# Moving the sampled rows' output projection into the tail of the convolution, with earlier weight loads, moved threshold steps and a moved first chunk

## The reference, cut to what matters

```
# layer 0
xn = rms_norm(y) ; q, k, v, iq, ik, iw, gate = split(xn @ att_w_in)
score = sum_h iw * relu(iq . ik) ; idx = top_k(score, 256)      # threshold search for the prompt rows,
o = softmax(q . k[idx]) @ v[idx]                                 # repeated extraction of 8 for the sampled rows
y = y + (o * silu(gate)) @ att_w_out                             # 1024 x 1024
# layer 1
xn = rms_norm(y) ; qkv, z, b, a = split(xn @ dn_w_in)            # 1024 x (3072 + 1024 + 16)
qkv = silu(conv4([state_dn_conv, qkv]))                          # new_buf is its last three rows
o = gated_delta_rule(qkv, g(a), beta(b), S0)
y = y + (rms_norm(o) * silu(z)) @ dn_w_out
```

## Time and profile before

| | us |
|---|---|
| three timed runs | 2287.26, 2297.11, 2298.11 (median 2297.11) |
| profiled execution, its own time | 2285.91 |
| its span | 2284.1 |
| TensorE busy in the span | 2100.2 (92%) |
| granted TensorE clock, mean | 0.956 |
| stage 1160.0 to 1673.8: span, TensorE busy | 513.8, 495.6 |
| stage 1673.8 to 1770.2: span, TensorE busy | 96.4, 83.6 |

### The profile page before, as it was taken

The page is one execution under the profiler, slowest core; times in us unless marked ns, Lnnn a source line. Parts: engine busy times, 40 slices in busy tenths (PEclk is TensorE's granted clock), DMA queues, the critical chain, the costliest instruction groups (busy, mean ns, idle before and its releaser), DMA issues. The chain is left out here.

```text
span 2284.1 us, 25198 instructions
## 1 busy us (share of the span) xinstructions
PE 2100.2 (92%) x9095; PEld 1273.4 (56%) x9095; DVE 1407.5 (62%) x2469; ACT 677.4 (30%) x1693; POOL 508.1 (22%) x529
## 2 busy tenths in 40 slices
PE   6979999999978899989889999999969899999997
PEld 5534543444444566655434556766523787777774
DVE  2558987599987887848876332223313576666662
ACT  3435641121222333321102222221101434433441
POOL 2111100000000000001111577777000413322320
PEclk9999999999989999999999999999979789999998
DMA  4024312101133212011112344445265642232210
GB/s 130 12 76 147 101 55 105 35 23 46 46 123 117 74 47 83 27 69 56 66 50 83 108 149 138 138 139 153 98 224 172 196 116 63 72 84 71 69 45 28
DMA packets 157827, 207.59 MB, mean 91 GB/s; under 512 B 43680, under 2 KB 107480, under 8 KB 157656
## 3 DMA queue, kind: packets, MB, share of 16 engines
q1 hardware_dynamic: 132436, 146.18, 19.9%
q0 software_dynamic: 16896, 50.35, 7.2%
q10 hardware_dynamic: 8372, 9.44, 1.2%
HBM read 162.19 MB, written 43.74 MB: 90 GB/s over the span
## 5 line engine op out<-in xcount | busy, mean ns | idle before, releaser
L1708 PE MATMUL acc_ch<-xnT,w_ch 128*128 128x512 f32 x768 | 357.5, 614 | 0.0
L1708 PEld LDWEIGHTS acc_ch<-xnT,w_ch 128*128 128x128 f32 x768 | 144.5, 196 | 155.7 <-issue 155.4
L791 PE MATMUL acc<-w_qg,xnT 128*128 128x512 f32 (+1 forms) x432 | 190.0, 593 | 0.0
L1597 POOL DMA_INDIRECT kg<-in_cache_k,rowidx x128 | 132.0, 1031 | 140.2 <-DVE rowidx L1856 81.4
L949 DVE MAX8 top_v<-scores 128x8 f32<-128x4100 f32 x32 | 141.7, 4428 | 0.7
L951 DVE FIND_INDEX8 top_i<-top_v,scores 128x8 uint32<-128x4100 f32 x32 | 141.5, 4423 | 0.0
L953 DVE MATCH_REPLACE8 scores<-top_v,scores 128x4100 f32<-128x4100 f32 x32 | 141.2, 4413 | 0.0
L1604 POOL DMA_INDIRECT vg<-in_cache_v,rowidx x128 | 127.4, 995 | 39.0 <-issue 33.2
L2663 PE MATMUL PB<-w_out_dn,ogT_dn 128*128 128x512 f32 x288 | 129.5, 604 | 4.0 <-DVE rhs L2927 3.3
L791 PE MATMUL acc<-w_kvq,xnT 128*128 128x512 f32 (+1 forms) x288 | 128.3, 604 | 4.6 <-PEq L543 4.6
L791 PEld LDWEIGHTS acc<-w_qg,xnT 128*128 128x128 f32 (+1 forms) x432 | 77.4, 184 | 96.6 <-issue 96.6
(11 more groups left out here) (417 smaller groups left out, 3778.1 us busy)
## 6 DMA issues: line engine op xcount, KB each, us to landing
w_ch<-in_dn_w_in SPq DMA_DIRECT2D x24, 512.0 KB, 5.0
qkv_d<-y_ch SPq DMA_DIRECT2D x24, 512.0 KB, 5.8
qkv_t<-qkv_d SPq DMA_DIRECT2D x8, 1536.0 KB, 8.0
w_ch_s<-in_dn_w_in SPq DMA_DIRECT2D x5, 2048.0 KB, 8.3
x<-in_x_all SPq DMA_DIRECT2D x9, 512.0 KB, 3.6
out_y_all<-y_t SPq DMA_DIRECT2D x9, 512.0 KB, 2.6
w_z_s<-in_dn_w_in ACTq DMA_DIRECT2D x1, 4160.0 KB, 30.6
w_kvq<-in_att_w_in SPq DMA_DIRECT2D x2, 2048.0 KB, 11.0
```

What stands on the lines that cost most here:

```text
L791: ins = pe.matmul(acc[rows(n), k % ACC, :], xnT[:, kk, cols(n)], w[:, kk, :], start=(kk == 0), stop=(kk == KT - 1))
L1597: pool.indirect_dma_start(kg[:, j % KR, :], None, ck, bass.IndirectOffsetOnAxis(ap=rowidx[:, u % 2, t * QT + u // 2:t * QT + u // 2 + 1], ...
L1708: ins = pe.matmul(acc[:, s, :], w[:, c % WR, k, :], xT[:, k, s * 512:(s + 1) * 512], start=(k == 0), stop=(k == KT - 1))
```

## The change

- `TOPK_IN`: 11 units stand in the late block of `index_project` (4 to 15) where 8 stood, 62 in `sample_scores` (15 to 77) where 63 stood, 13 and 12 in `head_project` (77 to 90, 90 to 102). In `index_project` the late block stands before `norm_ik(8)`, the last tile's, where it stood before the sums of the third trio.
- `NX_B` is 75: 37 extraction steps in `prompt_attend`, 21 in `dn_inputs`.
- `head_project`: no slot ahead of the last tile's norms; 12 slots where there were 13.
- The first chunk of the convolution's projection is issued at the end of `dn_inputs`' TensorE list; its accumulator `acc_ch` and its semaphore are shared, and `dn_inputs`' transposes use the same bank.
- `conv_attend`: the sampled rows' two output projections stand at the end of TensorE's list, around the last transpose. Their weights (two halves of 2 MB), the sampled rows of x, and the first two pieces of dn_w_in (2 MB each) are loaded by SP in this stage, into buffers that lie where gathered K and V rows and other tensors were (`home`, `kg`, `y_t0`), so SP waits until those have been read. The two pieces stand between stores 21 and 22.
- `dn_sample`: the output projection and those loads are gone; VectorE's add waits for the shared semaphores.

```diff
-TOPK_IN = {"index": (0, 4), "index_late": (4, 12), "sample_scores": (12, 75), "heads": (75, 89), "heads_late": (89, 102)}
+TOPK_IN = {"index": (0, 4), "index_late": (4, 15), "sample_scores": (15, 77), "heads": (77, 90), "heads_late": (90, 102)}
-NX_P, NX_B = 38, 73
+NX_P, NX_B = 38, 75
@@ index_project, VectorE
                     if n + 3 < NT:
                         norm_x(n + 3)
+                    if n == NT - 2:
+                        topk(*TOPK_IN["index_late"])
...
-                    if r == 2:
-                        topk(*TOPK_IN["index_late"])
@@ head_project, VectorE
-            parts, (u0, u1) = 2 * (m - 2) - 1, TOPK_IN["heads_late"]
+            parts, (u0, u1) = 2 * (m - 3), TOPK_IN["heads_late"]
...
-                beside(k)
+                if n < m - 1:
+                    beside(k)
                 norms(n)
@@ dn_inputs, TensorE, at its end
+            pe.wait_ge(w_in[0], 16)
+            for s in range(2):
+                for k in range(KT):
+                    ins = pe.matmul(acc_ch[:, s, :], w_ch[:, 0, k, :], xT[:, k, s * 512:(s + 1) * 512], start=(k == 0), stop=(k == KT - 1))
+                ins.then_inc(mm_ch, 1)
@@ conv_attend, SP
                 if c == NCH - WR:
-                    sp.dma_start(keep["w_out_s"][:], d["att_w_out"]...[:, :, 0:512]).then_inc(env["stores"]["wo_s_in"], 16)
+                    sp.wait_ge(kT_done, NK)
+                    for a in range(2):
+                        sp.dma_start(wo[a], d["att_w_out"]...[:, :, a * 512:(a + 1) * 512]).then_inc(wo_in[a], 16)
+                    sp.wait_ge(gT_done, 1)
+                    sp.dma_start(keep["y_t0"][:], d["x_all"][0:P, :]).then_inc(xs_in, 16)
...
-            for c in range(NCH - 3, NCH):
-                store(c)
+            store(NCH - 3)
+            sp.wait_ge(v_read, NK)
+            for a in range(2):
+                sp.dma_start(ws[:, a, :, :], d["dn_w_in"]...[:, :, a * 512:(a + 1) * 512]).then_inc(ws_in[a], 16)
+            store(NCH - 2)
+            store(NCH - 1)
@@ conv_attend, TensorE
-            for c in range(NCH):
+            for c in range(1, NCH):
...
+            def sample_out(c):
+                pe.wait_ge(o_ok, NQT)
+                pe.wait_ge(wo_in[c], 16)
+                pe.wait_ge(x_ok, 2 * (NCH - 1) + c + 1)
+                for h in range(H):
+                    ins = pe.matmul(acc[0:NS, c, :], og[:, h, :], wo[c][:, h, :], start=(h == 0), stop=(h == H - 1))
+                ins.then_inc(ys_done, 1)
+            sample_out(0)
             pe.wait_ge(tail_ok, NCH)
             pe.transpose(lgt[0:3 * NCH, 0:P], tail[:]...).then_inc(tail_t, 1)
+            sample_out(1)
@@ dn_sample, SP
-            sp.dma_start(wo[1][:], d["att_w_out"]...).then_inc(wo_in[1], 16)
-            sp.dma_start(x[:], d["x_all"][0:P, :]).then_inc(in_, 16)
...
-            load(1)
             for n in range(2, CONV // 512):
                 sp.wait_ge(mm, n - 1)
-                load(n)
+                sp.dma_start(w[:, n % 2, :, :], wv[:, :, n * 512:(n + 1) * 512]).then_inc(w_in[n % 2], 16)
@@ dn_sample, TensorE
-            out_proj(0)
             pe.wait_ge(cb_in, 16)
...
-            out_proj(1).then_inc(y_done, 1)
@@ dn_sample, ScalarE
-            act.dma_start(w[:, 0, :, :], wv[:, :, 0:512]).then_inc(w_in[0], 16)
@@ dn_sample, VectorE
-            dve.wait_ge(y_done, 1)
-            dve.wait_ge(in_, 16)
+            dve.wait_ge(ys_done, 2)
+            dve.wait_ge(xs_in, 16)
```

More of the change, by code:

```diff
@@ L1297, in dn_inputs @@
         mhalf = sb("mhalf_dn", [P, 1])
-        tpb = ctx.enter_context(nc.psum_tensor("tp_dn", [P, 2, 4, P], F32))
+        acc_ch, mm_ch = keep["acc_ch"], env["mm_ch"]
+        tpb = acc_ch[:].rearrange("p a (b c) -> p a b c", b=4)
         acc = ctx.enter_context(nc.psum_tensor("acc_dn", [P, 6, 512], F32))
@@ L1514, in conv_attend @@
         kg = sb("kg", [P, KR, 256])
-        vg = sb("vg", [P, VR, 256])
+        vg = keep["home"][:].rearrange("p (r e) -> p r e", e=256)
         ktg = sb("ktg", [P, 2, 2, P])
         vnew = sb("vnew", [32, NQT, HD])
-        gnat = sb("gnat", [NS, DM])
+        gnat = keep["y_t0"][0:NS, :]
+        wo = [keep["w_out_s"][:], kg[:].rearrange("p r e -> p (r e)").rearrange("p (h n) -> p h n", h=H)]
+        ws = keep["home"][:].rearrange("p (a k n) -> p a k n", a=2, k=KT)
+        wo_in, ws_in = ([env["stores"][f"{k}{i}"] for i in range(2)] for k in ("wo_s_in", "ws_in"))
+        xs_in, ys_done = env["stores"]["xs_in"], env["stores"]["ys_done"]
         gT = sb("gT", [P, H, NS])
@@ L1534, in conv_attend @@
         ga, gb, ach = sem("g_act"), sem("g_dve"), sem("g_chain_act")
-        cw_t, cw_ok, zero_ok, mm, x_ok, tail_ok, tail_t, nb_ok, conv_ok, th_ok, silu_ok = (
-            sem("ch_" + s) for s in ("cw_t", "cw_ok", "zero_ok", "mm", "x_ok", "tail_ok", "tail_t", "nb_ok", "conv_ok", "th_ok", "silu_ok"))
+        cw_t, cw_ok, zero_ok, x_ok, tail_ok, tail_t, nb_ok, conv_ok, th_ok, silu_ok = (
+            sem("ch_" + s) for s in ("cw_t", "cw_ok", "zero_ok", "x_ok", "tail_ok", "tail_t", "nb_ok", "conv_ok", "th_ok", "silu_ok"))
         st = [env["stores"][f"qkv_out{u}"] for u in range(YR)]
@@ L1576, in _ @@
                 if c == NCH - WR:
-                    sp.dma_start(keep["w_out_s"][:], d["att_w_out"].rearrange("l (h p) n -> p (l h) n", p=P)[:, :, 0:512]).then_inc(env["stores"]["wo_s_in"], 16)
+                    sp.wait_ge(kT_done, NK)
+                    for a in range(2):
+                        sp.dma_start(wo[a], d["att_w_out"].rearrange("l (h p) n -> p (l h) n", p=P)[:, :, a * 512:(a + 1) * 512]).then_inc(wo_in[a], 16)
+                    sp.wait_ge(gT_done, 1)
+                    sp.dma_start(keep["y_t0"][:], d["x_all"][0:P, :]).then_inc(xs_in, 16)
                 if c >= 3:
                     store(c - 3)
-            for c in range(NCH - 3, NCH):
-                store(c)
+            store(NCH - 3)
+            sp.wait_ge(v_read, NK)
+            for a in range(2):
+                sp.dma_start(ws[:, a, :, :], d["dn_w_in"].rearrange("l (k p) n -> p (l k) n", p=P)[:, :, a * 512:(a + 1) * 512]).then_inc(ws_in[a], 16)
+            store(NCH - 2)
+            store(NCH - 1)
             sp.wait_ge(nb_ok, 1)
@@ L1976, in sem @@
             return new_sem(nc, env, "sm_" + name)
-        wo = [keep["w_out_s"], sb("w_out_att_s", [P, H, 512])]
         wz = sb("w_z_s", [P, KT, 1040])
-        w = sb("w_ch_s", [P, 2, KT, 512])
+        w = keep["home"][:].rearrange("p (a k n) -> p a k n", a=2, k=KT)
         x, th = keep["y_t0"], keep["gz_t0"]
@@ L2004, in dn_sample @@
         beta, g = keep["beta"], keep["g"]
-        wo_in, in_, once = [env["stores"]["wo_s_in"], sem("wo_in")], sem("in"), sem("once")
+        once = sem("once")
         wz_in, cb_in = sem("wz_in"), sem("cb_in")
-        w_in = [sem("w_in0"), sem("w_in1")]
-        y_done, y_ok, ss_ok, rs_ok, xn_ok, tp_done, xT_ok = (sem(s) for s in ("y_done", "y_ok", "ss_ok", "rs_ok", "xn_ok", "tp_done", "xT_ok"))
+        w_in = [env["stores"]["ws_in0"], env["stores"]["ws_in1"]]
+        xs_in, ys_done = env["stores"]["xs_in"], env["stores"]["ys_done"]
+        y_ok, ss_ok, rs_ok, xn_ok, tp_done, xT_ok = (sem(s) for s in ("y_ok", "ss_ok", "rs_ok", "xn_ok", "tp_done", "xT_ok"))
         z_done, ba_done, th_ok, z_rd, gz_ok, ba_ok = (sem(s) for s in ("z_done", "ba_done", "th_ok", "z_rd", "gz_ok", "ba_ok"))
@@ L2057, in _ @@
         def _(pe):
-            def out_proj(c):
-                pe.wait_ge(wo_in[c], 16)
-                for h in range(H):
-                    ins = pe.matmul(yp[0:NS, c, :], og[:, h, :], wo[c][:, h, :], start=(h == 0), stop=(h == H - 1))
-                return ins
-            out_proj(0)
             pe.wait_ge(cb_in, 16)
@@ L3062, in build @@
         env["w_ch_in"] = [new_sem(nc, env, f"w_ch_in{i}") for i in range(WR)]
-        env["cw_in"] = new_sem(nc, env, "cw_in")
+        env["cw_in"], env["mm_ch"] = new_sem(nc, env, "cw_in"), new_sem(nc, env, "ch_mm")
         sampled = ctx.enter_context(ExitStack())
-        keep["w_out_s"] = sampled.enter_context(nc.sbuf_tensor("w_out_s", [P, H, 512], F32))
+        for name, shape in (("w_out_s", [P, H, 512]), ("home", [P, H * DM]), ("y_t0", [P, DM])):
+            keep[name] = sampled.enter_context(nc.sbuf_tensor(name, shape, F32))
+        ch_psum = ctx.enter_context(ExitStack())
+        keep["acc_ch"] = ch_psum.enter_context(nc.psum_tensor("acc_ch", [P, 2, 512], F32))
         with ExitStack() as both:
@@ L3074, in build @@
         clear_sems(nc, env)
-        for name, shape in (("qkv_t0", [P, 3 * H, P]), ("gz_t0", [P, DM]), ("y_t0", [P, DM]), ("tri", [P, 2, P]), ("blk", [P, 2, P]), ("m1c", [P, 2, P]),
+        for name, shape in (("qkv_t0", [P, 3 * H, P]), ("gz_t0", [P, DM]), ("tri", [P, 2, P]), ("blk", [P, 2, P]), ("m1c", [P, 2, P]),
                             ("m2c", [P, 2, P]), ("lev", [P, 7, P]), ("bsel", [P, DB]), ("i16", [H * NB, 256]), ("b16", [P, P])):
@@ L3078, in build @@
         dn_sample(nc, env)
```

(1 more changed line is left out.)

20 lines of the change are left out of this document (8 added, 12 removed).

## The result

The changed kernel's median is 2268.5 us over 13 runs (2263.5 to 2286.17), the kernel before on the same chip 2293.82 over 13 (2280.14 to 2298.9): a ratio of 0.9908 with a 95% interval of 0.9883 to 0.9932. The prediction was 2274, range 2258 to 2288. The medians lie 25.3 us apart. The profiled execution has a span of 2261.7 against 2284.1, 22.4 less, where the sum said 20.3.

The account below looks back on a forecast made before the run. The prediction took TensorE, busy 92% of the span, as the bound: time is gained where it idles and lost where it waits. Terms summing to -20.3 us off the mean of 2294.2 gave 2274, range 2258 to 2288.

Parts of the forecast that it names:

- Index, -11.7: Index stage: threshold steps issued before the last norm free TensorE's last score group from its wait; -11.7 us.
- The margin of 1.4 us: Index stage: eleven steps end at 133.4, the last norm's input comes at 134.8, leaving 1.4 us of cover.
- Sample scores, +0.4: sample_scores: ends on VectorE's steps, loses three of 1.72 us and gains two of 2.79; +0.4 us.
- Head, +1: Head projection: 12 fuller slots delay the gates, eating the gain at the last tile's norms; +1 us (-2.8 to +4).
- The two stalls I worked out: Head projection: gates behind fuller slots free TensorE's buffers late for tiles 6 and 7, about 3.6 us each.
- Attend, +5: prompt_attend: two more extraction steps of 4.43 us lengthen TensorE's waits; +5 us (+1.6 to +8.9).
- dn_inputs and first chunk, -2.5: dn_inputs to convolution start: two steps fewer and chunk 0 in idle time, limited by VectorE's chain; -2.5 us (-4.4 to 0).
- the stage ends 1.5 later for it: dn_inputs: chunk 0's 32 matmuls, queued where TensorE stood 9.41 us idle, end the stage 1.5 us later.
- Tail, -14 and +1.5: Convolution's end and dn_sample: first dn_w_in projection 14 us early, third weight piece behind w_z_s costs 1.5; -12.5 us.
- Both projections were at half clock: Old dn_sample: output projections took 9.9 us per 16 matmuls; behind the last chunk they would take 7.0 each.
- Rival C: dn_sample bound by transfers: state rows land late, weight pieces wait for w_z_s; -12.8, about 2281 us; chance 0.15.
- rival D: conv_attend's end: dn_w_in loads ahead of stores 22 and 23 delay the block; +14.4, 2309 us; chance 0.04.

Follow-up runs that it names:

- run 1: The kernel before with only the index edit: the late block's eight threshold steps ahead of the last tile's key norm; 2279.22 us, ratio 0.9936.
- run 12: The changed kernel with 15 threshold steps instead of 11 in the index stage's late block, four taken from sample_scores; 2273.64 us, ratio 0.9904.
- Run 8: The changed kernel with head_project's 13 slots as before, one ahead of the last tile's norms; 2330.35 us, ratio 0.9891.
- run 2: The changed kernel with NX_B back at 73: 35 extraction steps in prompt_attend, 23 in dn_inputs; 2272.92 us, ratio 0.99.
- run 5: The changed kernel with the first chunk of the convolution's projection back at the head of conv_attend; 2333.82 us, ratio 0.9893.
- run 11: The changed kernel plus split merge wait, early state rows and gain with square first, and 13 head slots, but first chunk back in conv_attend; 2253.59 us, ratio 0.9833.
- run 6: The changed kernel with VectorE's merge at the start of conv_attend waiting for the parity column alone, not 18 further loads; 2332.67 us, ratio 0.9892.
- run 3: The changed kernel with the sampled rows' two output projections at the head of dn_sample, all loads still early; 2281.7 us, ratio 0.9941.
- run 4: The changed kernel with the first two pieces of dn_w_in loaded at the start of dn_sample again; 2279.45 us, ratio 0.9924.

## Why the prediction was right, step by step

**Index, -11.7: -12.1.** Right, and shown alone by run 1. The margin of 1.4 us was 1.1. That each us beyond it costs one was too low: run 12 gives 8.3 for an overrun of 5.8.

**Sample scores, +0.4: +0.4.** Counted steps by counted durations.

**Head, +1: -0.8.** The two stalls I worked out (3.6 each) are there with 3.3 and 2.1; the sign of the whole was off by this difference. Run 8 shows that 13 slots would have been better, by 2.6 to 5.3.

**Attend, +5: +5.6.** That the two steps lengthen TensorE's waits is right: run 2 undoes it with -4.1, and the waits are back to 22.6 us. The size was luck: 5, between 3.2 and 8.9, was a choice and not a derivation, and the same text gave up to 10.7 in other executions.

**dn_inputs and first chunk, -2.5: -1.9.** The sum came out, the reasoning did not. I let TensorE's end move by 3 to 4.5 and the stage by 1.5 for the chunk, and gave the chunk the gain. Runs 5 and 11 take it apart. Without the chunk the stage would be 6.7 to 8.6 shorter, so the gain is in the two steps (run 2: 4.9), and the chunk eats 4 to 6 of it. The step that failed is "the stage ends 1.5 later for it". It kept the stage's end where it was while TensorE ended earlier; but the two steps fewer on VectorE bring that end forward as well (148.65 us in run 5 for 154.99 before), and with it 5.77 us of idle are left for the chunk and not 12 to 14. Set against that end, the chunk costs 8.5. Two errors of opposite sign cancelled, and that the sum came out is luck. The chain that sets the start of the convolution was named rightly, and run 6 shows it; I saw in it a limit on the gain, and not that VectorE would stand idle 14.2 us until the block starts.

**Tail, -14 and +1.5: -13.9 and +1.1.** The stage starts 15.4 us after the last chunk's end, as worked out, and the first projection 13.0 after that. The state rows are there 4.3 us after the start, between the 3.3 and 8.7 I had as ends; their transposes took 2.75 us instead of 1.67. The terms for the landing, transposes, copy and square add up to 11.1 and not to the 11.3 of the text, which changes nothing. "Both projections were at half clock" was read wrongly: at 9.9 us for 7.0 their granted clock was 0.70 and 0.71, so they ran in part at the lower level; the saving per projection was priced from the durations and came as priced. The gain has two sources, and run 3 divides it: 6.7 for the place in the list, 7.2 for the rest.

Rival C's collision did not come. The DMA engines were busy while w_z_s moved (0.99 of their time and 385 GB/s from 1672 to 1683), but it had landed 13.5 us after its issue at 1670.68, before SP issued the next piece at 1689.68. The rule of the Trainium skill (DMA: Bandwidth & Descriptors, "Issuing engines are not separate DMA queues"), that such loads share the same engines, agrees with run 4, where w_z_s took 24.9 us beside two pieces of 2 MB. For the rule of the Trainium skill that the prediction set beside rival D (same page, "Queues, rings and completion order"), no run here shows a store held up at a cost; store 22, behind two such pieces, landed after 5.1 us.

Outside my sum lie 2.5 us less between the page rows and chunk 23, within what the other kernels gave there (401.9 to 408.5 us on these two chips), and 1.5 more at the start.

## What to carry over

Before filling an engine's idle time at the end of a stage, ask which engine's chain opens the next one: work that delays the barrier delays that chain by as much, and may cost more than it saves (4 to 6 us in run 5, nothing in run 11, where the chain started sooner). Idle time that you want to fill must be measured with the other edits in place: 9.41 us had become 5.77 here. A wait for many small loads at the head of a chain is worth splitting (3.6 to 8.6 us here for one semaphore). Time parts by stretches between equal instructions: the sum agreed to 2 us here while one of its terms had two errors of several us that cancelled. And have more than one profile of a kernel before trusting a stretch: the same text differed by 5 us in attend.
